# A four-mixer decoder block: the first block of latent attention reordered, S5's powers and two low halves per layer on GpSimd

## What is computed

```python
def mla_mixer(h, positions, w_in, q_norm, kv_norm, w_q_up, w_kv_up, w_out):
    q_lat, kv_lat, k_pe, z = jnp.split(h @ w_in, [512, 1024, 1088], axis=-1)
    q = (rms_norm(q_lat, q_norm) @ w_q_up).reshape(bsz, T, 16, 128 + 64)
    kv = (rms_norm(kv_lat, kv_norm) @ w_kv_up).reshape(bsz, T, 16, 128 + 128)
    ...  # rotary embedding of q's last 64 columns and of k_pe, which all heads share
    o = causal_block_attention(q, k, v, 192 ** -0.5)
    return (o.reshape(bsz, T, 2048) * jax.nn.silu(z)) @ w_out

def s5_mixer(...):   # 128 groups of 16 channels, 64 complex states each
    step = jnp.exp(log_step)[:, None]
    lam_bar = jnp.exp(lam * step)
    b_bar = ((lam_bar - 1.0) / lam)[..., None] * complex(b_re, b_im)
    ...  # scan over time, output by c, skip, gelu, gate, silu(z), w_out
```

## Time and profile before

| | |
|---|---|
| median of 3 runs | 3800.28 us (3795.49 to 3802.94) |
| the profiled execution | 3803.58 us, its span 3801.9 us |
| TensorE busy | 3463.6 us, 91% of the span |
| VectorE busy | 2466.8 us, 65% |
| ScalarE busy | 1563.2 us, 41% |
| GpSimd busy | 142.3 us, 4% |
| mean granted clock of TensorE | 0.958 |

### The profile page before, as it was taken

One profiled execution on the slowest core, in us unless ns is written; L12 is line 12 of the kernel. 1 busy time (PEld: TensorE's weight loads), 2 busy tenths in 40 slices (PEclk: granted clock), 3 DMA queues, 4 the chain that ended last, 5 costly groups with the idle time before them and its releaser, 6 DMA issues.

```text
span 3801.9 us, 48707 instructions
## 1 busy us (share of the span) xinstructions
PE 3463.6 (91%) x18186; PEld 2957.4 (78%) x18186; DVE 2466.8 (65%) x3189; ACT 1563.2 (41%) x1853; POOL 142.3 (4%) x176
## 2 busy tenths in 40 slices
PE   5899999979999978888699999888998799999998
PEld 5777778767888867776599988777887688888886
DVE  4677777775555664554799976856556665665655
ACT  3344444434444333333367654333333344334342
POOL 0000000000000000000122200100000000000000
PEclk8899999989999988999899999999999999999999
DMA  5455555534444443333223245575665355455553
GB/s 209 155 188 188 192 194 188 194 140 182 177 178 175 166 161 122 124 130 111 98 104 112 99 144 207 173 226 217 223 224 193 133 192 187 177 196 188 185 186 126
DMA packets 89264, 642.83 MB, mean 169 GB/s; under 512 B 10176, under 2 KB 10256, under 8 KB 11712
## 3 DMA queue, kind: packets, MB, share of 16 engines
q1 hardware_dynamic: 83376, 607.16, 44.4%
q0 software_dynamic: 5776, 34.13, 2.8%
HBM read 638.02 MB, written 3.23 MB: 169 GB/s over the span
## 4 chain that ended last, share of the span: by engine, by line
PE 59%; DVE 18%; issue 7%; DVEq 6%; ACT 5%; DMA 4%; ACTq 0%; POOL 0%; SPq 0%; POOLq 0%
PE banks L682 16%; PE banks L683 16%; PE banks L684 16%; DVE WL L666 6%; DMA raw<-in_stream 4%; ACT WH L658 3%; DVE xc L1264 1%; PE banks L1409 1%; DVEq L2444 1%; PE banks L699 1%; DVEq L2434 1%; PE banks L700 1%; PE banks L701 1%; DVEq L1212 1%; PE banks L990 1%
## 5 line engine op out<-in xcount | busy, mean ns | idle before, releaser
L666 DVE TENSOR_TENSOR WL<-raw,WH 128x2048 fp32r<-128x2048 f32 (+2 forms) x575 | 1249.0, 2175 | 694.1 <-ACT WH L658 685.5
L658 ACT ACTIVATE WH<-raw 128x2048 fp32r<-128x2048 f32 (+2 forms) x575 | 1045.6, 1821 | 1070.8 <-DMA raw<-in_stream 518.0
L682 PE MATMUL banks<-WH,XH 128*128 128x512 f32 (+2 forms) x2784 | 1070.0, 384 | 72.9 <-DVE WL L666 33.2
L684 PE MATMUL banks<-WH,XL 128*128 128x512 f32 (+2 forms) x2784 | 1044.8, 375 | 0.0
L683 PE MATMUL banks<-WL,XH 128*128 128x512 f32 (+2 forms) x2784 | 1044.5, 375 | 0.0
L682 PEld LDWEIGHTS banks<-WH,XH 128*128 128x128 f32 x2784 | 535.7, 192 | 172.3 <-issue 60.9
L684 PEld LDWEIGHTS banks<-WH,XL 128*128 128x128 f32 x2784 | 534.7, 192 | 82.2
L683 PEld LDWEIGHTS banks<-WL,XH 128*128 128x128 f32 x2784 | 536.1, 193 | 77.9 <-issue 0.5
L682 PE MATMUL banks<-WH,YH 128*128 128x512 f32 x976 | 395.9, 406 | 13.4 <-DVE acc L779 8.5
L683 PE MATMUL banks<-WL,YH 128*128 128x512 f32 x976 | 390.6, 400 | 0.0
L684 PE MATMUL banks<-WH,YL 128*128 128x512 f32 x976 | 387.7, 397 | 0.0
(11 more groups left out here) (405 smaller groups left out, 3534.3 us busy)
## 6 DMA issues: line engine op xcount, KB each, us to landing
raw<-in_stream SPq DMA_DIRECT2D x575, 1024.0 KB, 4.8
gain<-in_gains POOLq DMA_DIRECT2D x9, 1024.0 KB, 5.1
arow<-acs_scratch POOLq DMA_DIRECT2D x8, 1024.0 KB, 5.0
offs<-in_ln_b POOLq DMA_DIRECT2D x4, 1024.0 KB, 7.3
acc<-in_x SPq DMA_DIRECT2D x2, 1024.0 KB, 6.6
src<-in_mem POOLq DMA_DIRECT2D x1, 2048.0 KB, 8.4
toep<-rvec_scratch POOLq DMA_DIRECT2D x4, 512.0 KB, 8.6
out_y<-src SPq DMA_DIRECT2D x2, 1024.0 KB, 3.9
```

The costliest lines, as they stand in the source:

```text
L658: nc.scalar.activation(WH[:, n.first % PARTS, at], raw[:, n.first % RAWS, at], ACT.Copy).then_inc(hi_ready, 1)
L666: nc.vector.tensor_tensor(WL[:, n.first % PARTS, at], raw[:, n.first % RAWS, at], WH[:, n.first % PARTS, at].bitcast(F32), ALU.subtract).t ...
L682: nc.tensor.matmul(out, xh[:, k0 + k, at], wh[:, k, lo:hi], start=start, stop=False)
L684: ins = nc.tensor.matmul(out, xl[:, k0 + k, at], wh[:, k, lo:hi], start=False, stop=stop)
```

## The change

In three parts. In MLA's first block the stream has three gate slots ahead of head 0's projection, and TensorE does them beside the latents' chain: one after the narrow slot, one around the latents' transposes, one before the key's last transposes. The block then gets an order of its own (`first_body`) with two of the four projections between the steps of heads 0 and 1. VectorE and ScalarE do slots 4 to 6 before the angles.

S5's discretisation moves to GpSimd (`s5_powers`), into the MLA layer. ScalarE's exponentials and sines for it, and VectorE's reciprocal, are done there too; its tiles lie in `small`, and `dt5`, `turns5` and `jump5` are given other memory. The scaling of the residual comes after S5's first tables.

At the start of FOX, MLA, S5, cross attention and feed forward, GpSimd does the first two slots' low halves (`first_lows`), between the powers of the norm's two halves. VectorE does the third slot's after the norm.

```diff
+        if b == 0:
+            gate(b, 0, 3)
+            up(0)
+            gate(b, 3, 4)
+            up(1)
+        else:
+            up(4 * b)
+            gate(b, 0, 3)
+            up(4 * b + 1)
+            gate(b, 3, 4)
             rows(w["mla_w_out"], (b - 1) * N, 4)
...
+    def first_lows(pool, slot, r):
+        pool.wait_ge(src_ready, 4 * (r - 1) + 2)
+        for n in range(slot, slot + 2):
+            pool.wait_ge(hi_ready, n + 1)
+            pool.wait_ge(lo_ready, n)
+            at = slice(0, slot_width(At(n)))
+            nc.gpsimd.tensor_tensor(WL[:, n % PARTS, at], raw[:, n % RAWS, at], WH[:, n % PARTS, at].bitcast(F32),
+                                    ALU.subtract).then_inc(lo_ready, 1)
...
         add_half(dve, slot, 1, 0)
-        split_low(dve, At(slot + 1 + LEAD))
         if i is not None:
             turn_low(dve, i, 0, 2)
         add_half(dve, slot, 1, 1)
-        split_low(dve, At(slot + 2 + LEAD))
         if i is not None:
             turn_low(dve, i, 2, 4)
-        split_low(dve, At(slot + 3 + LEAD))
         add_half(dve, slot, 1, 2)
         add_half(dve, slot, 1, 3)
         norm(dve, 1)
         if i is not None:
+            dve.wait_ge(lo_ready, slot + 3 + LEAD)
+            split_low(dve, At(slot + 3 + LEAD))
             turn_low(dve, i, 4, 6)
             split_low(dve, At(slot + 4 + LEAD), True)
...
+    def norm_powers(pool, slot=None, r=None):
         for tt in range(TT):
             served_pool[0] += 1
             power(pool, served_pool[0], tt, tt + 1)
+            if tt == 0 and slot is not None:
+                first_lows(pool, slot, r)
...
+        z = MLA_SLOT + 9
+        wait(pe, free[1], claims.claim(1))
+        products(pe, At(z), 4, N, 1, True, False)
         pe.wait_ge(kpe_rows, 1)
         for tt in range(TT):
             ins = nc.tensor.transpose(bank[4][:, tt * 64:tt * 64 + 64], kpeT[:, tt * P:tt * P + P], ident[0:64, 0:64])
         ins.then_inc(kpe_turned, 1)
+        products(pe, At(z + 1), 4, N, 1, False, False, k0=4, only=(0, 1), done=False)
...
+        products(pe, At(z + 1), 4, N, 1, False, False, k0=4, only=(2, 3))
+        products(pe, At(z + 2), 4, N, 1, False, False, k0=8)
         pe.wait_ge(latl_ready, 4)
         for tt in range(TT):
             ins = nc.tensor.transpose(bank[4][0:64, tt * P:tt * P + P], kper[:, tt, :], ident)
         ins.then_inc(kpeT_done, 1)
-        pe.wait_ge(rope_ready, 1)
...
+        def first_body(m):
+            up(At(z + 3), m, 0)
+            products(pe, At(z + 4), 4, N, 1, False, True, k0=12)
+            pe.wait_ge(rope_ready, 1)
+            turn_qk(pe, m, 0, "mla")
+            up(At(z + 5), m, 0)
+            scores(pe, m, "mla")
+            up(At(z + 6), m, 1)
+            turn_probs(pe, m, "mla")
+            up_queries(At(z + 7), 0)
+            values(pe, m, 0, "mla")
+            turn_qk(pe, m.plus(1), 1, "mla")
+            up_keys(At(z + 7), 0)
+            scores(pe, m.plus(1), "mla")
+            turn_head(pe, m)
+            turn_probs(pe, m.plus(1), "mla")
+            values(pe, m.plus(1), 1, "mla")
+            turn_qk(pe, m.plus(2), 0, "mla")
...
-        served_act[0] += 1
-        act.wait_ge(act_asked, served_act[0])
-        nc.scalar.activation(cossin[:, 1, :, :], ang[:, :, :], ACT.Sin)
-        nc.scalar.activation(cossin[:, 0, :, :], ang[:, :, :], ACT.Sin, scale=0.5).then_inc(act_done, 1)
         for j in range(2):
             for s in range(4):
                 split_high(act, At(MLA_SLOT + 4 * j + s + LEAD))
             evacuate(act, lat[:, j, :, :], j, At(MLA_SLOT + 4 * j + 3))
-        split_high(act, At(MLA_SLOT + 8 + LEAD))
+            if j == 0:
+                served_act[0] += 1
+                act.wait_ge(act_asked, served_act[0])
+                nc.scalar.activation(cossin[:, 1, :, :], ang[:, :, :], ACT.Sin)
+                nc.scalar.activation(cossin[:, 0, :, :], ang[:, :, :], ACT.Sin, scale=0.5).then_inc(act_done, 1)
+                act.wait_ge(par_loaded, 16)
+                nc.scalar.activation(tmp5[:, TMP, :], par5[:, LSTEP, :], ACT.Exp).then_inc(step_ready, 1)
         act.drain()
...
+        z = MLA_SLOT + 9
+        split_high(act, At(z + 2))
+        split_high(act, At(z + 3))
...
+        def first_body(m):
+            split_high(act, At(z + 4))
+            split_high(act, At(z + 5))
+            split_high(act, At(z + 6))
+            head_to_sbuf(act, m, 0, 0, At(z + 3), "mla")
+            split_high(act, At(z + 7))
+            evacuate(act, z4, 1, At(z + 4))
+            act.drain()
+            nc.scalar.activation(tz4, z4, ACT.Tanh, scale=0.5).then_inc(nat_ready, 1)
+            split_high(act, At(z + 8))
+            head_to_sbuf(act, m.plus(1), 1, 0, At(z + 5), "mla")
+            exponentials(act, m, "mla")
+            split_high(act, At(z + 9))
+            head_to_sbuf(act, m.plus(2), 0, 1, At(z + 6), "mla")
+            split_high(act, At(z + 10))
+            exponentials(act, m.plus(1), "mla")
+            head_high(act, m, 0, "mla")
+            head_to_sbuf(act, m.plus(3), 1, 0, At(z + 7), "mla")
...
+        first_body(At(MLA_HEAD))
+        act.wait_ge(theta_ready, 1)
+        nc.scalar.activation(tmp5[:, RADIUS, :], tmp5[:, RADIUS, :], ACT.Exp)
+        nc.scalar.activation(tmp5[:, SIN1, :], tmp5[:, THETA, :], ACT.Sin)
+        nc.scalar.activation(tmp5[:, SINH, :], tmp5[:, THETA, :], ACT.Sin, scale=0.5).then_inc(sines_ready, 1)
...
+        for s in range(4):
+            split_low(dve, At(MLA_SLOT + s + LEAD))
         nc.vector.tensor_copy(posf[:, :], angi[:, :])
         dve.drain()
         for tt in range(TT):
             nc.vector.tensor_scalar(ang[:, tt, :], con[:, C_FREQ:C_FREQ + 32], posf[:, tt:tt + 1], None, ALU.mult)
         dve.drain()
         whole_turns(dve, ang[:, :, :], angk[:, :, :]).then_inc(act_asked, 1)
+        for s in range(4, 6):
+            split_low(dve, At(MLA_SLOT + s + LEAD))
         dve.wait_ge(act_done, ask("act"))
         nc.vector.tensor_tensor(angk[:, :, :], cossin[:, 0, :, :], cossin[:, 0, :, :], ALU.mult)
         dve.drain()
         nc.vector.tensor_scalar(cossin[:, 0, :, :], angk[:, :, :], -2.0, 1.0, ALU.mult, ALU.add)
-        for s in range(8):
+        for s in range(6, 8):
             split_low(dve, At(MLA_SLOT + s + LEAD))
+        dve.wait_ge(par_loaded, 16)
+        nc.vector.tensor_tensor(tmp5[:, CRE, :], par5[:, LRE, :], par5[:, LRE, :], ALU.mult)
+        nc.vector.tensor_tensor(tmp5[:, CIM, :], par5[:, LIM, :], par5[:, LIM, :], ALU.mult)
+        dve.drain()
+        nc.vector.tensor_tensor(tmp5[:, CRE, :], tmp5[:, CRE, :], tmp5[:, CIM, :], ALU.add)
+        dve.drain()
+        nc.vector.reciprocal(tmp5[:, TMP2, :], tmp5[:, CRE, :]).then_inc(norm5_ready, 1)
         dve.wait_ge(slots_used, MLA_SLOT + 9)
         nc.vector.tensor_copy(kpeT[:, :], bank[5][0:64, 0:T]).then_inc(kpe_rows, 1)
-        split_low(dve, At(MLA_SLOT + 8 + LEAD))
...
+        def first_body(m):
+            split_low(dve, At(z + 4))
+            split_low(dve, At(z + 5))
+            split_low(dve, At(z + 6))
+            turn_and_copy(m, 0)
+            split_low(dve, At(z + 7))
+            gated(At(0))
+            logits(dve, m, "mla")
+            split_low(dve, At(z + 8))
+            probs_to_sbuf(dve, m, "mla")
+            head_output(dve, m, 0, "mla", 0)
+            turn_and_copy(m.plus(1), 1)
+            split_low(dve, At(z + 9))
+            logits(dve, m.plus(1), "mla")
+            split_low(dve, At(z + 10))
+            probs_to_sbuf(dve, m.plus(1), "mla")
+            head_low(dve, m, 0, "mla")
+            head_output(dve, m.plus(1), 1, "mla", 1)
+            turn_and_copy(m.plus(2), 0)
...
         input_tables(0)
         split_low(dve, At(n + 5))
         output_tables(0)
+        dve.wait_ge(xt_done, 32)
+        scale_residual(dve)
         split_low(dve, At(n + 6))
+        nc.vector.tensor_scalar(bg5[:, :], bg5[:, :], 0.5, None, ALU.mult)
+        for q in range(4):
+            at = slice(32 * q, 32 * q + 32)
+            nc.vector.tensor_copy(jump5[at, 32 * (3 - q):32 * (3 - q) + 32], ident[at, 32 * q:32 * q + 32])
+        dve.drain()
...
+    def s5_powers(pool):
+        par, tmp = par5, tmp5
+        pool.wait_ge(par_loaded, 16)
+        pool.wait_ge(step_ready, 1)
+        pool.wait_ge(norm5_ready, 1)
+        radius, theta, turn, part = tmp[:, RADIUS, :], tmp[:, THETA, :], tmp[:, CRE, :], tmp[:, CIM, :]
+        nc.gpsimd.tensor_tensor(radius, par[:, LRE, :], tmp[:, TMP, :], ALU.mult)
+        nc.gpsimd.tensor_tensor(theta, par[:, LIM, :], tmp[:, TMP, :], ALU.mult)
+        pool.drain()
+        nc.gpsimd.tensor_scalar(turn, theta, 1 / TWO_PI, MAGIC, ALU.mult, ALU.add)
+        pool.drain()
+        nc.gpsimd.tensor_scalar(turn, turn, MAGIC, None, ALU.subtract)
+        for piece in (PI_1, PI_2, PI_3):
+            pool.drain()
+            nc.gpsimd.tensor_scalar(part, turn, piece, None, ALU.mult)
+            pool.drain()
```

(82 more changed lines are left out.)

242 lines of the change are left out of this document (95 added, 147 removed).

## The result

The changed kernel takes 3760.8 us (median of 4 runs, 3760.2 to 3762.8) against 3801.6 us (4 runs, 3795.5 to 3805.1): ratio 0.9893, 95% interval 0.9879 to 0.9907, 40.8 us less. The forecast was 3765. The profiled execution has a span of 3759.1 us at a mean granted clock of 0.967; before it was 3801.9 at 0.958. A second profile and more runs of the same kernel gave 3759.8 us, 0.9897 (0.9878 to 0.9917).

What follows compares the result with a forecast made beforehand. TensorE, busy 91% of the span, bounds the kernel; time is won where it stands still or its clock falls behind. -17 + 1.5 - 21.4 + 1.5 = -35.4 us against 3803.6 gives 3768, forecast 3765 for the median; range 3753 to 3786.

Steps and rivals of the forecast that it cites:

- Part 1, -17 us: Latent attention's first block: gate and projection slots reordered to fill TensorE's waits; -17 us, bounds 0 and -26.
- my own terms: First latent block: durations of TensorE's steps in the new order, summed to a block end at 1477 instead of 1497.0.
- What I took off for the clock: First latent block: 3 us taken off the 20 us gain for stretches at the lower clock.
- Part 2, -21.4 us at S5's start: S5's powers on GpSimd: outputs start at 1891.0 instead of 1912.46, the 16.73 us wait goes; bounds -4.8 and -24.
- the norm's 4.8: S5's start: first product at 1846.9 instead of 1851.73 because the norm ends 6.5 us earlier; -4.8 us.
- VectorE's terms from 1870.5 on: S5's start: slot, output tables, scaling, slot and copies after the input tables bring the first scan to 1883.6.
- the price at the side, +1.5: Latent attention: small GpSimd operations beside VectorE, two more table loads and the first group cost +1.5 us, between 0 and +6.
- Part 3, +1.5 us for four starts at 4.7 us a half: Four layer starts besides S5: GpSimd's low halves take 4.7 us each; VectorE's gain is given back by order, +1.5 us.
- 0.3, 0.4, -0.3 and 1.0: Change in us at the starts of latent attention, forgetting attention, cross attention and feed forward.
- the twelve matmuls: Layer starts: the third slot's first 12 matmuls, ahead of the turns in TensorE's order, taken as 3.0 us.
- Each us above costs 2 us per start: Five layer starts: each us of a GpSimd half above 4.7 costs 2 us per start, 10 in all.

Runs made afterwards that it cites:

- part 1 alone: The kernel before with only the reordered first block of the latent attention put in; 3786.9 us, 0.9965.
- alone -16.9: The kernel before with only S5's parameters, exponentials and sines prepared early and its powers on GpSimd; 3785.3 us, 0.9961.
- part 3 alone: The kernel before with only two low halves taken by GpSimd at the start of five layers; 3796.0 us, 0.9986.
- parts 1 and 2 together: The changed kernel with all low halves on VectorE again; 3766.9 us, 0.9913 of the kernel before.
- the bare heads: The changed kernel with the two up-projections in the first head's chain put ahead of its turn; 3767.8 us, 0.9911 of the kernel before.
- the turns were moved too: The changed kernel with TensorE's turns of the norm's second half ahead of the third slot's first products at four layer starts; 3752.2 us, 0.9874.
- doubled halves: The changed kernel with GpSimd making each of its ten moved low halves twice; 3801.9 us, 1.0003 of the kernel before.

## Why the prediction came out right

**Part 1, -17 us: right.** Measured alone -17.0, in the changed kernel -16.3. The steps held: no wait before slot 5, 2.85 us for the latents (forecast 2.9), the last turn of the block sooner after the norm's first power. With part 1 alone it is 19.4 us sooner (143.30 for 162.69), where I had written 20; my own terms add up to 1477.6 to 1477.9 and not 1477, so to 19. What I took off for the clock was needed, but at another place, behind the block. In the changed kernel the turn is 23.6 us sooner (139.09), with the idle time of part 1 alone (20.2 and 20.1) and 4.3 us less busy time, and 5.0 go back up to the next turn. TensorE from the norm's first power to that turn, before and after:

```profile
1333.47:1496.16 162.69, 129.60 (x661) 0.87 0.38 142
```

```profile
1334.00:1473.09 139.09, 118.86 (x660) 0.97 0.47 171
```

Idle time fell by 12.9 us and busy time by 10.7, of the same work. Behind the block it goes the other way. From that turn to the next the kernel before has full clock, part 1 alone 0.89, for the same 109 matmuls:

```profile
1496.16:1516.86 20.70, 18.16 (x109) 1.00 0.37 134
```

```profile
1475.06:1498.20 23.14, 20.60 (x109) 0.89 0.24 91
```

2.4 us go back there, and from the next turn on the distance stays at 17.0 us to the layer's end.

**Part 2, -21.4 us at S5's start with the norm's 4.8: right.** Measured -22.8; alone -16.9 for 16.6, part 3 alone -4.6 for 4.8. The first product comes 22.3 us after the norm's first power (forecast 22.5), the outputs after 65.3 (66.6), 57.2 us after the last turns of the norm's first half begin (58.5 by the forecast's times), and VectorE is late by 2.85 us (2.6). It was right because each next thing to be late was worked out in turn. One slip stands in the sum: VectorE's terms from 1870.5 on add up to 1882.7 and not 1883.6 for the first scan. It began 57.9 us after the norm's first power, by the slipped sum 59.2, by the terms 58.3; so 0.9 of the 1.4 us by which S5's start gave more is this slip. Too high was the price at the side, +1.5: between part 1 alone and parts 1 and 2 together it is 0.0. In the loop it does cost for a while: the wait for a rotated query behind the first block is 2.16 us with parts 1 and 2 and 1.19 with part 1 alone, and small operations on GpSimd last up to 2.37 us beside a split; at the layer's end nothing of it is left. With the old block it was 3.7.

**Part 3, +1.5 us for four starts at 4.7 us a half: right in the halves and the path, wrong in the clock, and near in the sum by luck.** The halves take 4.5 to 4.6 us, the norm at the latent attention ends at 1353.1 (forecast 1353.0), and the turns wait for the third low half as I had it. But counted from the norm's first power they start 1.1 us later than before at the latent attention, 2.3 at the forgetting attention, 2.5 at cross attention and 4.0 at feed forward: 9.8 us where I had 0.3, 0.4, -0.3 and 1.0. I had given the twelve matmuls between the wait for the low half and the turns 3.0 us, as at full clock. They take 4.4, and 5.3 at cross attention, at a granted clock of 0.62 to 0.50. And yet the stretches of the four starts change by only +0.3 us in the run of part 3 alone, and by +2.5 from the changed kernel without part 3 to the one with it. What I left out besides is the clock behind the turns. The forgetting attention, before and after:

```profile
845.50 1.97 PE L821 MATMUL banks<-con,acc 128*128 128x128 f32 x8 [4.28 <-DVE acc L913]
848.03 0.79 PE L682 MATMUL banks<-WH,XH 128*128 128x512 f32 x1 [0.56 <-DVE XL L839]
...
853.31 0.80 PE L821 MATMUL banks<-con,acc 128*128 128x128 f32 x4
```

```profile
844.45 0.77 PE L705 MATMUL banks<-WH,XH 128*128 128x512 f32 x1 [5.45 <-DVE WL L679]
...
848.85 1.03 PE L844 MATMUL banks<-con,acc 128*128 128x128 f32 x8
850.86 0.50 PE L705 MATMUL banks<-WH,XH 128*128 128x512 f32 x1 [0.98 <-DVE XL L862]
...
853.72 0.60 PE L844 MATMUL banks<-con,acc 128*128 128x128 f32 x4
```

In the kernel before TensorE comes out of its wait into the turns, and the twelve matmuls behind them run at a granted clock of 0.50 for 5.28 us. In the changed kernel the long wait stands earlier, and the same twelve run at 1.00 for 2.86 us. Over the four starts they take 11.4 us and not 19.8. The two errors, each about the clock behind a wait, nearly cancel. "Each us above costs 2 us per start": I reckoned +47, measured +42, of which 36 can be followed in the stretches.

**The remaining 4 us.** Forecast -35.4, measured -40.8 and -39.3. S5's start gave 1.4 more and part 2's side cost 1.5 less; about 2 may be the untouched stretch, which no run settles. The rest is within the spread of the kernel before, whose 17 runs on one chip go from 3795.6 to 3807.4.

What the runs corrected in the reasoning is the same thing twice, and the sum hid it: I counted waits by their length and not by the clock behind them. At the four starts the two errors cancelled; in the heads, where I counted cover by its waits alone, I expected the bare heads to cost nothing.

## What to carry to other kernels

Price a wait of TensorE by its length and by what it does to the granted clock behind it: up to the last turn of the first block 10.7 of 23.6 us were matmuls that ran faster. Then look whether that arrives: of the 39.1 us that the two stretches won it is 8.0, and the rest of S5 had 10.7 us less busy time and was hardly shorter. Follow work moved to another engine to the next thing TensorE waits for in its own order; two moved halves won the norm 4 to 7 us and TensorE nothing at four of five starts, until the turns were moved too. And cut both traces at the same events: two stretches held 39 of 43 us, and a second profile of each kernel showed which differences come without any change.

## What the hardware showed beyond that

An instruction of one column can be held for all that is left of a large one: the square of the mean at the feed forward's norm (128x1, two inputs in SBUF) takes 0.16 us in the kernel after. In the one with doubled halves it takes 2.17, up to 3031.18, and the GpSimd half that it met ends at 3031.17. First after, then the doubled kernel:

```profile
2991.60 0.16 DVE L943 TENSOR_TENSOR powin<-mv 128x1 f32<-128x1 f32 x1
```

```profile
3026.60 4.57 POOL L689 TENSOR_TENSOR WL<-raw,WH 128x2048 fp32r<-128x2048 f32 x1
...
3029.01 2.17 DVE L946 TENSOR_TENSOR powin<-mv 128x1 f32<-128x1 f32 x1
```

GpSimd pays too. Its power of one column took 0.54 us in the doubled kernel at 1368.01, when VectorE stood still, and in the kernel after, beside a scaling with two inputs in SBUF (1822.48 to 1825.12):

```profile
1822.81 1.53 POOL L958 TENSOR_TENSOR powout<-powin,con 128x1 f32<-128x1 f32 x1
```
